# Memory attention: probabilities times values as three f32r products, values split on GpSimd, probabilities on VectorE

## The chip, the core and the metric

The kernel runs on one core of a Trainium2 chip. The metric is the device time of one execution in microseconds (us); a median of several executions is compared. The engines that matter are TensorE (PE in the profile, its weight loads PEld), VectorE (DVE), ScalarE (ACT), GpSimd (POOL) and the queue of SyncE (SPq), which issues the loads of weights. Each runs its own list of instructions in order and waits on semaphores for the others.

## What is computed

Two transformer stacks run one after the other on 256 tokens of width 1024, all in float32. The first has two layers; each is a gated FFN, a mixer with three attention branches whose outputs are gated and merged, and another FFN. The change concerns the memory branch of the mixer: four heads of width 128 attend to 256 memory rows.

```python
def _memory_attention(q, k, v):
    z = jnp.einsum('bhqd,bhkd->bhqk', q, k).astype(jnp.float32) * (q.shape[-1] ** -0.5)
    p = jax.nn.softmax(z, axis=-1)
    return jnp.einsum('bhqk,bhkd->bhqd', p.astype(v.dtype), v)

# in each layer, beside a stick-breaking branch (o_sb) and a forgetting branch (o_fx) of eight heads each
g_sb, g_fx, g_mem = jnp.split(jax.nn.sigmoid(u @ w_gate[l] + b_gate[l]), N_BRANCH, axis=-1)
merged = (g_sb * (_merge_heads(o_sb) @ w_br_sb[l])
          + g_fx * (_merge_heads(o_fx) @ w_br_fox[l])
          + g_mem * (_merge_heads(o_mem) @ w_br_mem[l]))
```

## The kernel before

**Weights.** Every weight matrix streams from memory once, in chunks of up to 128x1024 float32. SyncE loads a chunk into one of four buffers `raw`; ScalarE copies it, rounded to float32r (f32r), into one of six slots `whi` (L578), and VectorE writes the remainder raw - whi into `wlo` (L1103). TensorE then takes three f32r products, high by high, high by low and low by high, in place of one product in full float32. `split_to(c)` marks in ScalarE's and VectorE's lists up to which chunk they have split. A slot is free when TensorE has used its chunk (`w_used`), a raw buffer when VectorE has written wlo.

**The mixer.** For each layer the values V come first, then `NPAIR` = 4 steps, called pairs here (two stick-breaking heads, two forgetting heads and one memory head each), eight in all for two layers. In a pair TensorE does, in this order: feature_chunk(0) and the memory scores (L2040), feature_chunk(1) and (2), the stick-breaking scores, feature_chunk(3), the turned memory probabilities into bank 7 (L1757), gate_chunk(0, 0), the forgetting scores, gate_chunk(0, 1), **probabilities times values** (L2074), gate_chunk(0, 2) and (0, 3), the running sums of the stick-breaking branch (L2086 to L2090), gate_chunk(1, 0) to (1, 3) with the turned forgetting probabilities between, and the outputs of the other two branches. gate_chunk(x, i) writes banks 0 and 1; gate_chunk(1, 0) waits for `gate_done`, that is for VectorE's L1309, which takes the gate of x = 0 out of these banks and adds the bias from `gbias`.

**The places that the change touches.** The memory probabilities are copied out of bank 7 by ScalarE into `mem_pT` (L757), and TensorE multiplies them in full float32 by `vmem`, the values kept in SBUF, for each of the two halves of 128 memory rows (L2074). On VectorE stand around that time `sb_w` (L1356), a weight split, the forgetting scores `fx_s` (L1363), their maxima (L1367), a split, `olo` (L1297), the reciprocal (L1371) of sums that ScalarE's exponentials (L767) yield, the normalisation (L1376), and the gates (L1309). GpSimd masks `sb_sp` (L550), subtracts `sb_lo` (L552) and masks `sb_w` (L554). At the start of a mixer VectorE writes two scaled blocks of ones (L1271, shown as gates) that TensorE turns; GpSimd fills three tiles (L546). SyncE loads a gate bias ahead of each four gate chunks (L469), into three buffers in turn.

The order is that in which each engine's code is written; no scheduler moves it.

Of the kernel before, what the change touches and what calls it, by code (L numbers as in the profile page):

```python
# [7 lines left out]
F32 = mybir.dt.float32  # L8
F32R = mybir.dt.float32r
BF16 = mybir.dt.bfloat16  # L10
ACT = mybir.ActivationFunctionType
ALU = mybir.AluOpType
# [94 lines left out]
def program(nc, A, consts, out):  # L107
    ctx = ExitStack()
    with ctx:
        def sb(name, shape, dt=F32, scope=ctx):  # L110
            return scope.enter_context(nc.sbuf_tensor(name, shape, dt))

        def sem(name):
            return ctx.enter_context(nc.semaphore(name))
# [78 lines left out]
        with ExitStack() as o:  # L193
            ohi, olo = sb("ohi", [P, 3 * NPAIR, TOK], F32R, o), sb("olo", [P, 3 * NPAIR, TOK], F32R, o)
            sb_hi, sb_lo = sb("sb_hi", [P, 2, CAUSAL], F32R, o), sb("sb_lo", [P, 2, CAUSAL], F32R, o)
            exact_r = sb("exact_r", [P, 2 * P], F32R, o)
            with ExitStack() as i:
                sb_e, sb_sp = sb("sb_e", [P, 2, CAUSAL], F32, i), sb("sb_sp", [P, 2, CAUSAL], F32, i)
                sb_w, fx_s = sb("sb_w", [P, 2, CAUSAL], F32, i), sb("fx_s", [P, 2, CAUSAL], F32, i)
                gates = sb("gates", [P, TT, 3 * DM], F32, i)  # L200
                mem_p, mem_pT = sb("mem_p", [P, 512], F32, i), sb("mem_pT", [P, 512], F32, i)
                qs, ks = sb("qs", [P, TOK], F32, i), sb("ks", [P, TOK], F32, i)
                qx = [sb(f"qx{h}", [P, TOK], F32, i) for h in range(2)]
                kx = [sb(f"kx{h}", [P, TOK], F32, i) for h in range(2)]
                crow = sb("crow", [P, TOK], F32, i)
                rstd_bc = sb("rstd_bc", [P, TOK], F32, i)
                V = sb("V", [P, TT, 3 * VB], F32, i)
                gbias = [sb(f"gbias{n}", [P, GB], F32, i) for n in range(3)]
            with ExitStack() as i:
                M = sb("M", [P, TT, DM], F32, i)  # L210
        rb = gates[:, 1, 2 * DM:2 * DM + TT * P].rearrange("p (t n) -> p t n", t=TT)
# [66 lines left out]
        qr0_full, qr_raw, qr_rot, qr_done, qrT_full, qr_ready = (  # L278
            sem(n) for n in ("qr0_full", "qr_raw", "qr_rot", "qr_done", "qrT_full", "qr_ready"))
        group_done = sem("group_done")  # L280
        ls_full, ls_add, ls_max, ls_exp, ls_rec, ls_norm, ls_tp, ls_pt = (
            sem(n) for n in ("ls_full", "ls_add", "ls_max", "ls_exp", "ls_rec", "ls_norm", "ls_tp", "ls_pt"))
        la_full, la_hi, la_lo = sem("la_full"), sem("la_hi"), sem("la_lo")
        y_out, y_stored = sem("y_out"), sem("y_stored")

# [45 lines left out]
        def _(sp):  # L331
# [111 lines left out]
            for l in range(LAYERS):  # L443
                ffn(2 * l, skip=4 if l == 0 else 0)
                if l == 0:
                    for m in range(LAYERS):
                        w = A["w_mem_kv"][m]
                        for n in range(4):
                            load(c_mem + 8 * m + n, cols(w, KT, n * P, P))
                        for j in range(4):  # L450
                            load(c_mem + 8 * m + 4 + j, moving(w, 2 * j, [(MH * P, MH * P)]))
                w = A["w_in"][l]
                v_at = [[(1024, VB)], [(1024 + VB, 512 - VB), (2560, 2 * VB - 512)], [(2560 + 2 * VB - 512, VB)]]
                for i in range(12):
                    load(c_v[l] + i, moving(w, 2 * (i % 4), v_at[i // 4]))
                for h in range(MH):
                    load(c_qm[l] + h, cols(w, KT, 3080 + h * P, P))
                load_gain(3 * l + 1, A["mix_post_g"][l])
                wg = A["w_gate"][l]
                for p in range(NPAIR):  # L460
                    c = c_pair_[l] + 12 * p
                    for n, part_at in enumerate((0, 512, 1536, 2048)):
                        load(c + n, cols(w, KT, part_at + p * P, P))
                    for x in range(2):
                        j = l * 8 + 2 * p + x
                        at = (2 * p + x) * GB
                        if j >= 3:
                            sp.wait_ge(gate_done, 2 * (j - 3) + 2)
                        sp.dma_start(gbias[j % 3][:, :], A["b_gate"][l, at:at + GB].partition_broadcast(P)).then_inc(gb_loaded, 16)  # L469
                        for i in range(4):  # L470
                            load(c + 4 + 4 * x + i, moving(wg, 2 * i, [(at, GB)]))
                wb = [A[n][l] for n in ("w_br_sb", "w_br_fox", "w_br_mem")]
                for i, br in enumerate(BRANCHES):
                    for k in range(4):
                        load(c_br[l] + 4 * i + k, rows_of(wb[br], k))
                for k in range(KT):
                    load(c_wo[l] + k, rows_of(A["w_out"][l], k))
                ffn(2 * l + 1)
# [51 lines left out]
        @block.gpsimd  # L530
        def _(pool):
            diag = lambda t: t[:, :, :].rearrange("p h (a n) -> p h a n", n=P)[:, :, 0:3:2, :]
            mask = before.unsqueeze(1).unsqueeze(1).to_broadcast([P, 2, 2, P])

            def ffn(f):
                for n in range(2, FT):
                    pool.wait_ge(chi_done, wide(f, n) + 1)
                    pool.tensor_tensor(hlo[:, n, :], hid_f[n % 2][:, :], hhi[:, n, :].bitcast(F32), ALU.subtract).then_inc(clo_done, 1)  # L538

            pool.wait_ge(cst_loaded, 32)  # L540
            for l in range(LAYERS):

                ffn(2 * l)
                pool.wait_ge(v_done, 6 * l + 1)
                for n, (tile, value) in enumerate(((qx[0], 1.0), (qx[1], 1.0), (kx[1], 0.0))):
                    pool.memset(tile[:, :], value).then_inc(fx_rows, 1)  # L546
                for p in range(NPAIR):
                    I = l * NPAIR + p
                    pool.wait_ge(sb_dve, I * 2 + 2)
                    pool.tensor_tensor(diag(sb_sp), diag(sb_sp), mask, ALU.mult).then_inc(sb_masked, 1)  # L550
                    pool.wait_ge(sb_high, I + 1)
                    pool.tensor_tensor(sb_lo[:, :, :], sb_sp[:, :, :], sb_hi[:, :, :].bitcast(F32), ALU.subtract).then_inc(sb_split, 1)  # L552
                    pool.wait_ge(sb_exp, I + 1)
                    pool.tensor_tensor(diag(sb_w), diag(sb_w), mask, ALU.mult).then_inc(sb_ready, 1)  # L554
                ffn(2 * l + 1)
            for use in range(2):
                for f in range(FT):
                    pool.wait_ge(chi_done, conv_tile(use, f) + 1)
                    pool.tensor_tensor(hlo[:, f, :], hf[f % 2][:, :], hhi[:, f, :].bitcast(F32), ALU.subtract).then_inc(clo_done, 1)
# [3 lines left out]
        def _(act):  # L563
# [448 lines left out]

            def mla_pT(h):
                act.wait_ge(ls_tp, h + 1)
                act.activation(lpT[h % 4][:, :], bank[4 + h % 2][:, 0:CAUSAL], ACT.Copy).then_inc(ls_pt, 1)

            def mla_high(h):
                act.wait_ge(la_full, h + 1)
# [76 lines left out]
        def _(dve):  # L1095
# [170 lines left out]
            def mixer(l):  # L1266
# [33 lines left out]
                def take_gate(p, x):  # L1300
                    j = l * 8 + 2 * p + x
                    at = (2 * p + x) * GB
                    dve.wait_ge(gb_loaded, 16 * (j + 1))
                    for t in range(TT):
                        if t == 0:
                            dve.wait_ge(gt0_full, j + 1)
                        else:
                            dve.wait_ge(w_used, c_pair_[l] + 12 * p + 8 + 4 * x)
                        dve.scalar_tensor_tensor(gates[:, t, at:at + GB], bank[t][:, 0:GB], stat(b, t, RSTD), gbias[j % 3][:, :],  # L1309
                                                 ALU.mult, ALU.add).then_inc(gate_done, 1)  # L1310

                for p in range(NPAIR):
# [42 lines left out]
                    for h in range(2):  # L1355
                        ins = dve.tensor_tensor(sb_w[:, h, :], bank[2 + h][:, 0:CAUSAL], sb_sp[:, h, :], ALU.subtract)  # L1356
                    ins.then_inc(sb_dve, 1)
                    split_to(c + 3 + SLOTS)

                    dve.wait_ge(fxz_full, I + 1)  # L1360
# [360 lines left out]
        def _(pe):  # L1721
# [223 lines left out]
            def mixer(l):  # L1945
# [66 lines left out]
                for p in range(NPAIR):  # L2012
# [56 lines left out]
                        ins = pe.matmul(bank[4 + h][:, P:CAUSAL], qx[h][r, P:TOK], kx[h][r, 0:TOK], start=True, stop=True)  # L2069
                    ins.then_inc(fxz_full, 1)  # L2070
                    gate_chunk(0, 1)
                    pe.wait_ge(mem_pt, I + 1)
                    for k in range(TT):
                        ins = pe.matmul(bank[6][:, 0:TOK], vmem[l][:, k, p * P:(p + 1) * P], mem_pT[:, k * TOK:(k + 1) * TOK],  # L2074
                                        start=(k == 0), stop=(k == TT - 1))
                    ins.then_inc(o_full[MEM], 1)
                    gate_chunk(0, 2)
                    gate_chunk(0, 3)
# [223 lines left out]
                ins.then_inc(ls_tp, 1)  # L2302

            def mla_values(h):
                pe.wait_ge(ls_pt, h + 1)
                if h >= 2:
                    pe.wait_ge(la_lo, h - 1)
                d = bank[6 + h % 2]
# [116 lines left out]
```

## Time and profile before

| | us |
|---|---|
| median of 3 runs | 1848.41 |
| range of these runs | 1848.38 to 1849.37 |
| the profiled execution | 1848.37 |
| its span, first to last instruction | 1846.6 |

The profile is of one execution. Busy time is the sum over an engine's instructions. A timeline row gives start, duration, engine, line, operation, tiles and count; "x2" joins two instructions that follow each other. In brackets stands how long the engine had been idle and what ended that. TensorE's matmuls overlap, since their durations include the way through the array; what one costs is the step from start to start. A float32 product that isn't f32r shows as two records for one instruction. The granted clock is 1.000 over the whole run, TensorE's level of 2.4 GHz.

### The profile page before, as it was taken

To read this page: it belongs to the slowest core of one execution; us is meant where nothing else is said; L and a number is where in the kernel's file an instruction comes from. 1 tells how busy PE (TensorE), PEld (TensorE's weight loads), DVE (VectorE), ACT (ScalarE), POOL (GpSimd) and SP (SyncE) were. 2 spreads that over 40 slices of the span, in tenths; PEclk is the share of its full clock that TensorE was granted. 3 is DMA by queue.
4 is the path that set the end of the run, shared out by engine and by line. 5 is a ranking of instruction groups with operands and counts; after the bars stand their busy time and mean duration, and the time that the engine had idled before them with its cause. 6 is when DMAs were issued, how large, how long until landed. Compare 5 with 4: busy or idle time off the path is not lost.

```text
span 1846.6 us, 28820 instructions
## 1 busy us (share of the span) xinstructions
PE 1829.8 (99%) x10951; PEld 1633.7 (88%) x10951; DVE 1287.2 (70%) x2040; ACT 1090.1 (59%) x1884; POOL 205.9 (11%) x158
## 2 busy tenths in 40 slices
PE   8999999999999999999999999999999999999998
PEld 7888899998888888888999888888889998889997
DVE  6775747787777567755777778755768765768863
ACT  7665545556666466645555657655557655757653
POOL 0220001110022002200011102210002210001210
PEclk9999999999999999999999999999999999999999
DMA  9765575455576558655654548654747664536753
GB/s 269 208 188 183 168 198 171 140 156 177 171 225 192 189 150 232 186 192 141 191 179 141 188 146 230 190 194 145 220 139 217 190 198 152 176 103 198 204 192 103
DMA packets 435721, 333.94 MB, mean 181 GB/s; under 512 B 25338, under 2 KB 381312, under 8 KB 435584
## 3 DMA queue, kind: packets, MB, share of 16 engines
q1 hardware_dynamic: 435008, 331.57, 59.8%
q8 instruction: 87, 1.43, 0.3%
q10 hardware_dynamic: 576, 0.53, 0.1%
q14 instruction: 50, 0.41, 0.1%
HBM read 330.97 MB, written 1.05 MB: 180 GB/s over the span
## 4 chain that ended last, share of the span: by engine, by line
PE 95%; DVE 2%; ACT 1%; DMA 1%; issue 0%; ACTq 0%; SPq 0%
PE bank L1751 16%; PE bank L1728 14%; PE bank L1730 14%; PE bank L1729 14%; PE bank L1739 7%; PE bank L1741 7%; PE bank L1740 7%; PE bank L1753 7%; PE bank L1757 2%; PE bank L1750 1%; DVE wlo L1103 1%; DVE U L1156 1%; PE bank L2003 0%; PE bank L2069 0%; PE bank L2074 0%
## 5 line engine op out<-in xcount | busy, mean ns | idle before, releaser
L1103 DVE TENSOR_TENSOR wlo<-raw,whi 128x1024 fp32r<-128x1024 f32 (+3 forms) x638 | 761.7, 1201 | 289.6 <-ACT whi L578 280.2
L578 ACT ACTIVATE whi<-raw 128x1024 fp32r<-128x1024 f32 (+3 forms) x638 | 647.0, 1023 | 330.4 <-PE bank L1730 244.8
L1751 PE MATMUL bank<-U,whi 128*128 128x512 f32 x1280 | 438.4, 395 | 0.2 <-DVE wlo L1103 0.2
L1753 PE MATMUL bank<-U,wlo 128*128 128x256 f32 x1120 | 314.6, 281 | 0.0
L1739 PE MATMUL bank<-U,whi 128*128 128x256 f32 x1024 | 289.2, 282 | 0.0
L1741 PE MATMUL bank<-U,wlo 128*128 128x256 f32 x1024 | 286.3, 280 | 0.0
L1740 PE MATMUL bank<-U,whi 128*128 128x256 f32 x1024 | 285.7, 279 | 0.0
L1751 PEld LDWEIGHTS bank<-U,whi 128*128 128x128 f32 x1280 | 229.9, 188 | 42.9 <-DVE wlo L1103 0.7
L1728 PE MATMUL bank<-whi,U 128*128 128x384 f32 (+2 forms) x592 | 219.3, 370 | 2.8 <-DVE U L1156 2.0
L1728 PE MATMUL bank<-whi,hhi 128*128 128x512 f32 x560 | 219.3, 392 | 0.0
L1730 PE MATMUL bank<-wlo,hhi 128*128 128x512 f32 x560 | 218.1, 389 | 0.0
L1729 PE MATMUL bank<-whi,hlo 128*128 128x512 f32 x560 | 217.9, 389 | 0.0
L1753 PEld LDWEIGHTS bank<-U,wlo 128*128 128x128 f32 x1120 | 210.1, 188 | 7.0
L1730 PE MATMUL bank<-wlo,U 128*128 128x384 f32 (+2 forms) x592 | 211.3, 357 | 0.0
L1729 PE MATMUL bank<-whi,U 128*128 128x384 f32 (+2 forms) x592 | 211.2, 357 | 0.0
L1739 PEld LDWEIGHTS bank<-U,whi 128*128 128x128 f32 x1024 | 192.0, 188 | 2.8 <-issue 1.5
L1740 PEld LDWEIGHTS bank<-U,whi 128*128 128x128 f32 x1024 | 192.7, 188 | 0.3
L1741 PEld LDWEIGHTS bank<-U,wlo 128*128 128x128 f32 x1024 | 192.4, 188 | 0.0
L538 POOL TENSOR_TENSOR hlo<-hid_f,hhi 128x256 fp32r<-128x256 f32 x80 | 108.3, 1353 | 598.9 <-ACT hhi L654 598.9
L1730 PEld LDWEIGHTS bank<-wlo,hhi 128*128 128x128 f32 x560 | 105.1, 188 | 22.2
L1729 PEld LDWEIGHTS bank<-whi,hlo 128*128 128x128 f32 x560 | 105.2, 188 | 21.3
L1728 PEld LDWEIGHTS bank<-whi,hhi 128*128 128x128 f32 x560 | 105.1, 188 | 21.0
(307 smaller groups left out, 2365.1 us busy)
## 6 DMA issues: line engine op xcount, KB each, us to landing
raw<-in_ffn_w_up SPq DMA_DIRECT2D x351, 256.0 KB, 3.5
raw<-in_ffn_w_down SPq DMA_DIRECT2D x264, 256.0 KB, 2.9
raw<-in_ffn_w_gate SPq DMA_DIRECT2D x175, 256.0 KB, 3.4
raw<-in_w_gate SPq DMA_DIRECT2D x128, 192.0 KB, 3.0
raw<-in_w_in SPq DMA_DIRECT2D x80, 256.0 KB, 3.5
raw<-in_a_w_in SPq DMA_DIRECT2D x48, 256.0 KB, 3.3
raw<-in_w_mem_kv SPq DMA_DIRECT2D x32, 256.0 KB, 3.3
raw<-in_w_out SPq DMA_DIRECT2D x32, 256.0 KB, 3.0
```

The lines of the kernel that those rows point to most:

```text
L538: pool.tensor_tensor(hlo[:, n, :], hid_f[n % 2][:, :], hhi[:, n, :].bitcast(F32), ALU.subtract).then_inc(clo_done, 1)
L578: act.activation(whi[n % SLOTS][:, 0:w], raw[n % RAW][:, 0:w], ACT.Copy).then_inc(hi_ready, 1)
L1103: dve.tensor_tensor(wlo[n % SLOTS][:, 0:w], raw[n % RAW][:, 0:w], whi[n % SLOTS][:, 0:w].bitcast(F32), ALU.subtract).then_inc(lo_ready, 1)
L1728: pe.matmul(dst, xh, wh, start=start, stop=False)
L1729: pe.matmul(dst, xl, wh, start=False, stop=False)
L1730: return pe.matmul(dst, xh, wl, start=False, stop=stop)
L1739: pe.matmul(dst, wh, xh[:, k, :], start=(k == 0), stop=False, skip_group_check=skip)
L1740: pe.matmul(dst, wh, xl[:, k, :], start=False, stop=False, skip_group_check=skip)
L1741: ins = pe.matmul(dst, wl, xh[:, k, :], start=False, stop=(k == kts - 1), skip_group_check=skip)
L1751: ins = pe.matmul(dst, wh, u2[:, k, :], start=(k == 0), stop=(k == KT - 1))
L1753: pe.matmul(dst[:, 0:TOK], wl, uhi[:, k, :], start=False, stop=False)
L1757: return pe.transpose(dst, src, ident)
```

## The change

The values of a pair are split by GpSimd: `vm_hi` is vmem rounded to f32r, `vm_lo` the remainder. It does that ahead of the pair's first mask, when the previous pair's product has been taken. ScalarE now writes `mem_pT` as f32r, and VectorE writes the remainder of the probabilities, bank 7 - mem_pT, into `mem_pl`, between sb_w and the weight split that follows. TensorE takes three f32r products for each half in place of one float32 product, and waits for both splits. To make room, mem_pl lies where mem_p lies, and there are two gate bias buffers in place of three, so that a bias load waits for the gate two before and not three before. A semaphore is reused for the second stack (mem_pt for ls_pt).

```diff
-                mem_p, mem_pT = sb("mem_p", [P, 512], F32, i), sb("mem_pT", [P, 512], F32, i)
+                with ExitStack() as k:
+                    mem_p = sb("mem_p", [P, 512], F32, k)
+                mem_pl, mem_pT = sb("mem_pl", [P, 512], F32R, i), sb("mem_pT", [P, 512], F32R, i)
...
-                gbias = [sb(f"gbias{n}", [P, GB], F32, i) for n in range(3)]
+                gbias = [sb(f"gbias{n}", [P, GB], F32, i) for n in range(2)]
+                vm_hi, vm_lo = sb("vm_hi", [P, TT, P], F32R, i), sb("vm_lo", [P, TT, P], F32R, i)
...
-                        if j >= 3:
-                            sp.wait_ge(gate_done, 2 * (j - 3) + 2)
-                        sp.dma_start(gbias[j % 3][:, :], A["b_gate"][l, at:at + GB].partition_broadcast(P)).then_inc(gb_loaded, 16)
+                        if j >= 2:
+                            sp.wait_ge(gate_done, 2 * (j - 2) + 2)
+                        sp.dma_start(gbias[j % 2][:, :], A["b_gate"][l, at:at + GB].partition_broadcast(P)).then_inc(gb_loaded, 16)
...
+                    pool.wait_ge(m_taken, 6 * LAYERS)
+                    if I > 0:
+                        pool.wait_ge(o_full[MEM], I)
+                    values = vmem[l][:, :, p * P:(p + 1) * P]
+                    pool.tensor_copy(vm_hi[:, :, :], values).then_inc(vm_split, 1)
+                    pool.wait_ge(vm_split, I * 2 + 1)
+                    pool.tensor_tensor(vm_lo[:, :, :], values, vm_hi[:, :, :].bitcast(F32), ALU.subtract).then_inc(vm_split, 1)
                     pool.wait_ge(sb_dve, I * 2 + 2)
...
                     ins.then_inc(sb_dve, 1)
+                    dve.wait_ge(mem_pt, I * 2 + 1)
+                    dve.tensor_tensor(mem_pl[:, :], bank[7][:, :], mem_pT[:, :].bitcast(F32), ALU.subtract).then_inc(mem_pt, 1)
                     split_to(c + 3 + SLOTS)
...
-                    pe.wait_ge(mem_pt, I + 1)
+                    pe.wait_ge(mem_pt, I * 2 + 2)
+                    pe.wait_ge(vm_split, I * 2 + 2)
                     for k in range(TT):
-                        ins = pe.matmul(bank[6][:, 0:TOK], vmem[l][:, k, p * P:(p + 1) * P], mem_pT[:, k * TOK:(k + 1) * TOK],
-                                        start=(k == 0), stop=(k == TT - 1))
+                        ph, pl = mem_pT[:, k * TOK:(k + 1) * TOK], mem_pl[:, k * TOK:(k + 1) * TOK]
+                        pe.matmul(bank[6][:, 0:TOK], vm_hi[:, k, :], ph, start=(k == 0), stop=False)
+                        pe.matmul(bank[6][:, 0:TOK], vm_hi[:, k, :], pl, start=False, stop=False)
+                        ins = pe.matmul(bank[6][:, 0:TOK], vm_lo[:, k, :], ph, start=False, stop=(k == TT - 1))
                     ins.then_inc(o_full[MEM], 1)
```

On VectorE, in each pair after sb_w. Before:

```order
L1356 TENSOR_TENSOR sb_w<-bank,sb_sp 128x384
L1103 TENSOR_TENSOR wlo<-raw,whi 128x768 [waits hi_ready]
L1363 SCALAR_TENSOR_TENSOR fx_s<-bank,ctok,cst 128x128 [waits fxz_full]
L1363 SCALAR_TENSOR_TENSOR fx_s<-bank,ctok,cst 128x256
L1367 TENSOR_REDUCE fmax<-fx_s 128x2 [waits fx_add]
```

The same place now, where all line numbers are ten or more higher:

```order
L1366 TENSOR_TENSOR sb_w<-bank,sb_sp 128x384
L1369 TENSOR_TENSOR mem_pl<-bank,mem_pT 128x512 [waits mem_pt]
L1113 TENSOR_TENSOR wlo<-raw,whi 128x768 [waits hi_ready]
L1375 SCALAR_TENSOR_TENSOR fx_s<-bank,ctok,cst 128x128 [waits fxz_full]
L1375 SCALAR_TENSOR_TENSOR fx_s<-bank,ctok,cst 128x256
```

One instruction, mem_pl, stands between sb_w and the split; GpSimd's mask waits for sb_w (sb_dve), so it no longer meets the split first.

On TensorE, between gate_chunk(0, 1) and (0, 2). Before:

```order
L1730 MATMUL bank<-wlo,U 128x384
L2074 MATMUL bank<-mem_pT,vmem 128x256 [waits mem_pt]
L2074 MATMUL bank<-mem_pT,vmem 128x256
L1728 MATMUL bank<-whi,U 128x384 [waits lo_ready]
L1729 MATMUL bank<-whi,U 128x384
```

Now:

```order
L1742 MATMUL bank<-wlo,U 128x384
L2088 MATMUL bank<-mem_pT,vm_hi 128x256 [waits vm_split,mem_pt]
L2089 MATMUL bank<-mem_pl,vm_hi 128x256
L2090 MATMUL bank<-mem_pT,vm_lo 128x256
L2088 MATMUL bank<-mem_pT,vm_hi 128x256
L2089 MATMUL bank<-mem_pl,vm_hi 128x256
L2090 MATMUL bank<-mem_pT,vm_lo 128x256
L1740 MATMUL bank<-whi,U 128x384 [waits lo_ready]
```

Two instructions have become six, with one more semaphore to wait for.

On GpSimd, at the start of a mixer. Before:

```order
L546 MEMSET kx 128x256
L550 TENSOR_TENSOR sb_sp<-sb_sp,cst 128x2x2x128 [waits sb_dve]
L552 TENSOR_TENSOR sb_lo<-sb_sp,sb_hi 128x768 [waits sb_high]
L554 TENSOR_TENSOR sb_w<-sb_w,cst 128x2x2x128 [waits sb_exp]
L550 TENSOR_TENSOR sb_sp<-sb_sp,cst 128x2x2x128 [waits sb_dve]
```

Now:

```order
L549 MEMSET kx 128x256
L556 CAST vm_hi<-vmem 128x256 [waits m_taken]
L558 TENSOR_TENSOR vm_lo<-vmem,vm_hi 128x256 [waits vm_split]
L560 TENSOR_TENSOR sb_sp<-sb_sp,cst 128x2x2x128 [waits sb_dve]
L562 TENSOR_TENSOR sb_lo<-sb_sp,sb_hi 128x768 [waits sb_high]
L564 TENSOR_TENSOR sb_w<-sb_w,cst 128x2x2x128 [waits sb_exp]
L556 CAST vm_hi<-vmem 128x256 [waits o_full2,m_taken]
```

The copy and the subtraction stand ahead of each pair's first mask, and so directly behind the previous pair's last one or behind the memsets.

## Rows read from the trace of the kernel before

**Rows 1.** The page's part 1, busy time, share and instructions per engine.

```profile
PE 1829.8 (99%) x10951; PEld 1633.7 (88%) x10951; DVE 1287.2 (70%) x2040; ACT 1090.1 (59%) x1884; POOL 205.9 (11%) x158
```

**Rows 2.** Timeline of TensorE, first pair (start us, duration us, engine, line, operation, tiles).

```profile
301.46 1.02 PE L2074 MATMUL bank<-mem_pT,vmem 128*128 128x256 f32 x4
302.14 0.53 PE L1728 MATMUL bank<-whi,U 128*128 128x384 f32 x1
302.50 0.34 PE L1729 MATMUL bank<-whi,U 128*128 128x384 f32 x1
302.68 0.34 PE L1730 MATMUL bank<-wlo,U 128*128 128x384 f32 x1
```

**Rows 3.** Timeline of TensorE: feature_chunk(2), first and last of 30 matmuls; gate_chunk(1, 0).

```profile
288.25 0.28 PE L1739 MATMUL bank<-U,whi 128*128 128x256 f32 x1
...
291.54 0.28 PE L1741 MATMUL bank<-U,wlo 128*128 128x256 f32 x1
...
307.51 0.35 PE L1728 MATMUL bank<-whi,U 128*128 128x384 f32 x1
```

**Rows 4.** Timeline of VectorE, first pair, from sb_w to the gates of x = 0.

```profile
298.68 1.02 DVE L1356 TENSOR_TENSOR sb_w<-bank,sb_sp 128x384 f32<-128x384 f32 x2
299.61 0.95 DVE L1103 TENSOR_TENSOR wlo<-raw,whi 128x768 fp32r<-128x768 f32 x1
300.48 1.39 DVE L1363 SCALAR_TENSOR_TENSOR fx_s<-bank,ctok,cst 128x128 f32<-128x128 f32 x4
...
302.83 2.48 DVE L1103 TENSOR_TENSOR wlo<-raw,whi 128x768 fp32r<-128x768 f32 x1
...
305.57 0.16 DVE L1371 RECIPROCAL frec<-fsum 128x4 f32<-128x4 f32 x1
...
306.69 1.14 DVE L1309 SCALAR_TENSOR_TENSOR gates<-bank,st,gbias 128x384 f32<-128x384 f32 x2
```

**Rows 5.** Timeline of GpSimd in the same stretch.

```profile
299.78 1.93 POOL L550 TENSOR_TENSOR sb_sp<-sb_sp,cst 128x512 f32<-128x512 f32 x1 [47.60 <-DVE sb_w L1356]
302.66 1.84 POOL L552 TENSOR_TENSOR sb_lo<-sb_sp,sb_hi 128x768 fp32r<-128x768 f32 x1 [0.95 <-ACT sb_hi L761]
```

**Rows 6.** Timeline of ScalarE: first and last row of the four exponentials.

```profile
302.95 0.41 ACT L767 ACTIVATE fx_s<-fx_s,fmax 128x128 f32<-128x128 f32 x1
...
304.63 0.19 ACT L767 ACTIVATION_READ_ACCUMULATOR fx_s<-fx_s,fmax 128x1 f32 x1
```

**Rows 7.** Timeline of VectorE between two stages: 128x512 with a bank as input.

```profile
857.85 0.69 DVE L1128 TENSOR_TENSOR bank<-bank,gpost 128x512 f32<-128x512 f32 x1
```

**Rows 8.** Instructions of L550, L554 and L559: durations in ns, least, median, most.

```profile
L550 POOL TENSOR_TENSOR sb_sp<-sb_sp,cst x8: 1926/1937/1937, 299.8 to 1018.0; 128x512 f32<-128x512 f32 x8
...
L554 POOL TENSOR_TENSOR sb_w<-sb_w,cst x8: 1327/1340/1342, 312.9 to 1031.1; 128x512 f32<-128x512 f32 x8
...
L559 POOL TENSOR_TENSOR hlo<-hf,hhi x44: 737/1276/1480, 1396.3 to 1785.3; 128x256 fp32r<-128x256 f32 x44
```

**Rows 9.** Timeline at the mixer start of layer 1: GpSimd, VectorE, TensorE.

```profile
866.47 0.31 POOL L546 MEMSET kx<- 128x256 f32 x1
...
866.61 1.66 DVE L1103 TENSOR_TENSOR wlo<-raw,whi 128x688 fp32r<-128x688 f32 x2 [2.36 <-ACT whi L578]
868.18 0.48 DVE L1271 TENSOR_SCALAR gates<-cst,st 128x128 f32<-128x128 f32 x2
...
868.72 0.44 PE L1757 MATMUL bank<-cst,gates 128*128 128x128 f32 x2 [0.72 <-DVE gates L1271]
```

**Rows 10.** Timeline of SyncE's queue around two bias loads, and VectorE's second gate.

```profile
309.68 0.50 SPq L469 DMA_DIRECT2D gbias<-in_b_gate  x1
...
316.15 0.43 SPq L469 DMA_DIRECT2D gbias<-in_b_gate  x1
318.23 10.01 SPq L337 DMA_DIRECT2D raw<-in_w_gate  x8
...
316.72 0.62 DVE L1309 SCALAR_TENSOR_TENSOR gates<-bank,st,gbias 128x384 f32<-128x384 f32 x1 [0.36 <-PE bank L1730]
```

More of the change, by code:

```diff
@@ L280, in program @@
         group_done = sem("group_done")
-        ls_full, ls_add, ls_max, ls_exp, ls_rec, ls_norm, ls_tp, ls_pt = (
-            sem(n) for n in ("ls_full", "ls_add", "ls_max", "ls_exp", "ls_rec", "ls_norm", "ls_tp", "ls_pt"))
+        ls_full, ls_add, ls_max, ls_exp, ls_rec, ls_norm, ls_tp, vm_split = (
+            sem(n) for n in ("ls_full", "ls_add", "ls_max", "ls_exp", "ls_rec", "ls_norm", "ls_tp", "vm_split"))
         la_full, la_hi, la_lo = sem("la_full"), sem("la_hi"), sem("la_lo")
@@ L1014, in mla_pT @@
                 act.wait_ge(ls_tp, h + 1)
-                act.activation(lpT[h % 4][:, :], bank[4 + h % 2][:, 0:CAUSAL], ACT.Copy).then_inc(ls_pt, 1)
+                act.activation(lpT[h % 4][:, :], bank[4 + h % 2][:, 0:CAUSAL], ACT.Copy).then_inc(mem_pt, 1)
             def mla_high(h):
@@ L1308, in take_gate @@
                             dve.wait_ge(w_used, c_pair_[l] + 12 * p + 8 + 4 * x)
-                        dve.scalar_tensor_tensor(gates[:, t, at:at + GB], bank[t][:, 0:GB], stat(b, t, RSTD), gbias[j % 3][:, :],
+                        dve.scalar_tensor_tensor(gates[:, t, at:at + GB], bank[t][:, 0:GB], stat(b, t, RSTD), gbias[j % 2][:, :],
                                                  ALU.mult, ALU.add).then_inc(gate_done, 1)
@@ L2304, in mla_values @@
             def mla_values(h):
-                pe.wait_ge(ls_pt, h + 1)
+                pe.wait_ge(mem_pt, 2 * LAYERS * NPAIR + h + 1)
                 if h >= 2:
```

## The prediction

> **What bounds the kernel now.** I read the page's busy times first. The reader is to see one engine that never rests: TensorE is busy 99% of the span, VectorE 70%, ScalarE 59%, GpSimd 11% [rows 1]. So only two things can move the time: what TensorE itself issues, and whether somebody makes it wait. Work added to VectorE or GpSimd is free until it makes one of TensorE's waits end later. For this I then read the timeline of TensorE, VectorE, GpSimd and ScalarE through the first head pair. The other seven pairs repeat it: the mask on GpSimd takes 1926 to 1937 ns in all eight [rows 8].
>
> **Removed and added on TensorE.** Two f32 products per pair appear as four records from 301.46; the next f32r matmul starts at 302.14, but the one after it only at 302.50, where the usual step is 0.18 us (302.50 to 302.68) [rows 2]. So the block costs 302.50 - 301.46 - 0.18 = 0.86 us. In its place stand six f32r matmuls of 256 columns. Thirty of that form stand in one feature chunk, with 29 steps from 288.25 to 291.54, so 0.113 us each [rows 3]; six cost 0.68 us. Saving: 0.18 us a pair, 8 x 0.18 = 1.4 us. The two semaphore waits ahead of them I put at nothing, as mem_pl and vm_hi/vm_lo are ready (next).
>
> **Are the operands ready?** mem_pl reads a bank and one SBUF tile, 128x512; the nearest row is L1128, 128x512 with a bank as input, 0.69 us [rows 7]. It starts where the weight split started, at 299.61, and ends at 300.30, 1.16 us before TensorE asks at 301.46 [rows 2, 4]. The wait for mem_pT in front of it has long ended. vm_hi and vm_lo are made right after the previous pair's last mask on GpSimd, more than ten microseconds before. Cost: nothing.
>
> **What mem_pl pushes back.** Here I expect the loss. Queued behind it on VectorE are a weight split (L1103), the forgetting scores (L1363), their maxima, a second split, the reciprocal and the gates (L1309), and TensorE waits for the first gate before gate_chunk(1, 0), which starts at 307.51 [rows 3]. Before, that gate starts at 306.69 [rows 4] and takes 0.62 us [rows 10], to 307.31: a slack of 0.20 us.
> Step by step, in times of the first pair:
> The first split would start at 299.61 + 0.69 - 0.09 = 300.21 (the next instruction starts 0.09 us ahead of an end: 298.68 + 1.02 against 299.61) [rows 4]. But GpSimd's mask has started at 299.78 [rows 5]. The trace shows what such a pair does: the second split, started at 302.83 while GpSimd subtracts from 302.66 to 304.50, takes 2.48 us in place of 0.95 and ends at 305.31, 0.81 us after GpSimd [rows 4, 5]. And the mask, which now starts 0.17 us behind a split, takes 1.93 us, while one of the same shape on L554 takes 1.34 [rows 5, 8]. So whoever is second stands still. Before, the split was first and GpSimd paid; with mem_pl between, GpSimd is first and VectorE pays. mem_pl itself holds nobody: the scores, also bank plus one SBUF tile, ran from 300.48 beside the mask, which still ended at 301.71.
> The Trainium skill says the same in "SBUF — State Buffer", section "Who interferes with whom": a VectorE instruction with two SBUF inputs and a reading GpSimd instruction exclude each other, and the one that issues first keeps the ports to its end. The trace agrees, with 2.48 us against 0.95.
> So the mask ends at 299.78 + 1.34 = 301.12, the split at 301.93, and the scores start at 301.85 in place of 300.48: 1.37 us late. The four exponentials on ScalarE follow the maxima at once, so they end at 304.63 + 0.19 + 1.37 = 306.19 [rows 6]. The second split is now free: sb_hi and GpSimd's subtraction run 0.59 us earlier and end at 303.91, ahead of the split at 304.20; it ends at 305.15. So the reciprocal waits for the exponentials, not for the split: 306.23 in place of 305.57, 0.66 us late. With it the gate comes at 307.35 and ends at 307.97, TensorE goes on at about 308.01. It arrives at 307.51 - 0.18 = 307.33. Stall: 0.68 us, of which the saving pays 0.18. Net +0.50 us a pair, 8 x 0.50 = +4.0 us.
> Half of the 1.37 us vanishes in slack that is there, since the second split stood still before; that is why the price isn't 1.37.
> What comes later in the pair (sb_w, the second gate, the next pair's first chunk) moves with TensorE's stall and has slack of its own.
>
> **GpSimd's two new instructions.** The subtraction of 128x256 takes 0.74 us at the least (L559's minimum) [rows 8]; the copy lies between the memset of the same size, 0.31 us [rows 9], and that; I take 0.5. In seven of eight pairs they run at the end of the pair before or on an idle engine, where the worst they do is hold a split that lies chunks ahead. At the mixer start of layer 1 it is different: GpSimd's memsets end at 866.78, VectorE runs two splits from 866.61 to 868.27, then the two L1271 that TensorE is already waiting for: it idles 0.72 us up to 868.72 [rows 9]. If the copy slips in between the splits and the subtraction ahead of L1271, these come up to 0.5 + 0.74 = 1.2 us later, all of it TensorE's. Bounds 0 and 1.2 us; I take 1.0, as a waiting GpSimd was served at the end of the split that held it [rows 5]. In layer 0 VectorE is idle at that place.
> On L1271 the rows show no meeting with GpSimd. The Trainium skill, same section, lists tensor_scalar among those that can contend; by it the bound of 1.2 us is reached, without it 0.5.
>
> **The two bias buffers.** SP's load of a bias now waits for the gate two before. For x = 0 that gate ends at about 308.5 with the delay, the load stands at 309.68: no wait. For x = 1 it ends at 316.72 + 0.62 = 317.34, the load stands at 316.15: SP stands 1.2 us, and with 0.43 us of issue is free at 317.77. Queued behind is the next weight load, which starts at 318.23 anyway, as its buffer is not free earlier [rows 10]. Cost: nothing, as long as the cover of 0.46 us holds; both sides move with TensorE's delay.
>
> **Sum.** The profiled execution has a span of 1846.6 us and took 1848.37, the median is 1848.41, so differences carry over. 1848.4 - 1.4 + 5.4 (8 x 0.68) + 1.0 = 1853.4 us.
>
> **Rivals.**
> Absorbed (not slower): the split isn't held by the mask, because VectorE gets the ports although GpSimd began 0.43 us before. Then it runs 300.21 to 301.16, the exponentials end at 305.42, the second split is held until 304.50 as before and ends at 305.31, the reciprocal stays at 305.57, the gate at 307.31 meets TensorE at 307.33. Only the saving is left: 1848.4 - 1.4 + 0 to 1.2, about 1847.6. For it: the slack really is as large as mem_pl's 0.60 us. Against: rows 4 and 5 show the hold in either direction.
> Larger loss: the hold lengthens, because GpSimd also waits for mem_pl and begins only at its end. Then the split ends 0.5 us later still, and since slack is used up all goes to TensorE: +4.0, 1857.4. Against: the scores ran beside the mask.
> The bias load becomes late: SP's wait passes 318.23 and weight loads slip until TensorE sees it. It decides from 0.46 us of further delay; at six or seven places of 0.5 us, 1857. Six weight slots lie between.
> Faster: the three products are worth more than the rows say. The whole block is 8 x 0.86 = 6.9 us, so 3.7 us would need a block of 0.40 us, six matmuls of 0.07. No row has that.
>
> **Chances.** Below 0.2% (3.7 us) a measurement of this kernel can't be told from no change. Main case 0.68, with a range of its own of 1851.2 (stall 0.5, start 0.2) to 1855.4 (stall 0.9, start 1.2); four fifths of it, 0.54, lie above 1852.1. Absorbed 0.22. Larger loss and late bias together 0.08. Faster 0.02. So slower 0.54 + 0.08 = 0.62, same 0.14 + 0.22 = 0.36, faster 0.02. The range takes in the main and the absorbed case, 1847.0 to 1856.0, and leaves out 0.1.
>
> **What would show it.** Right: the split behind mem_pl at about 1.7 us, the mask at 1.34 in place of 1.93, and some 0.7 us of TensorE idle ended by VectorE's gates at each gate_chunk(1, 0); the six matmuls in 0.68 us; TensorE's wait for L1271 in layer 1 near 1.7 us. Wrong: no idle time on TensorE at the gates, or idle time ahead of the six matmuls, or ended by a DMA.

## The result, and the profile after

The changed kernel takes 1854.11 us (median of 9 runs, 1853.61 to 1855.21) against 1848.91 us (9 runs, 1848.38 to 1850.31) of the kernel before on the same chip: ratio 1.0028, 95% interval 1.002 to 1.0036. It is 5.2 us slower; the forecast was 5.0 (1853.4 on a base of 1848.4 us, the median of the first three runs).

The head of the page of the changed kernel, its part 1, and the shares of its chain of work:

```profile
span 1852.4 us, 28891 instructions
```

```profile
PE 1830.7 (99%) x10967; PEld 1634.0 (88%) x10967; DVE 1286.7 (69%) x2048; ACT 1090.4 (59%) x1884; POOL 215.8 (12%) x174
```

```profile
PE 93%; DVE 3%; ACT 2%; issue 1%; DMA 1%; ACTq 0%; SPq 0%
```

Against [rows 1] TensorE is 0.9 us busier and the span 5.8 us longer. So the time isn't in what TensorE does but in what it waits for, and in the chain VectorE and ScalarE have one point more each than before (3% and 2% against 2% and 1%). Where, the table by stage shows. Each row is a stretch in us, its length, and the busy time (and instructions) of PE, PEld, DVE, ACT and POOL; then clock, DMA share and GB/s. Of the kernel before, the four pairs of layer 0, the mixer start of layer 1, and its four pairs:

```profile
285.35:425.67 140.32, 140.32 (x979) 135.38 (x977) 108.74 (x187) 77.40 (x141) 20.50 (x12) 1.00 0.53 160
855.25:896.01 40.76, 39.94 (x287) 39.02 (x286) 28.30 (x54) 27.22 (x53) 0.81 (x3) 1.00 0.79 219
896.01:1036.47 140.46, 140.46 (x979) 135.53 (x977) 108.53 (x187) 77.47 (x141) 20.49 (x12) 1.00 0.52 160
```

The same three stretches of the changed kernel:

```profile
285.44:428.24 142.80, 140.27 (x986) 135.10 (x984) 108.10 (x191) 77.37 (x141) 24.12 (x18) 1.00 0.52 156
857.79:899.24 41.45, 39.96 (x288) 39.05 (x287) 28.58 (x54) 27.03 (x53) 3.00 (x5) 1.00 0.76 208
899.24:1041.82 142.58, 140.08 (x987) 134.88 (x985) 108.38 (x192) 77.25 (x141) 24.12 (x18) 1.00 0.53 160
```

The pairs cost +2.48 and +2.12 us, together 4.60 or 0.58 a pair; the start of layer 1 costs +0.69. In the pairs before, TensorE was busy for the whole of the stretch; now 2.5 us of each are idle. The clock is 1.00 throughout. The remaining 0.5 us of the span lie in stages that the change doesn't touch: 0.09 us ahead of the first pair, and 0.45 us behind the last one (810.58 us to the end of the span in place of 810.13). Both come from one execution of each kernel.

The groups of waits of the changed kernel that matter (what stood and what ended it: us in all, times, the longest of them). Before, no row named the gates of the pairs, and the second one was 0.7 us:

```profile
PE bank L1740 <- DVE gates L1319: 5.0, 8, 0.7
...
PE bank L1769 <- DVE gates L1281: 1.4, 1, 1.4
...
SPq L472 <- DVE gates L1319: 8.0, 6, 1.3
```

Eight waits at gate_chunk(1, 0), one at the mixer start. SyncE's queue now stands 1.3 us at six bias loads (before, 1.3 us at four of them together). No wait of TensorE in the pairs is ended by a DMA; the only one in the run is that for the constants at its start, 2.7 us and 2.8 us before.

Timeline of VectorE in the first pair, from sb_w to the gates, which answers to [rows 4]:

```profile
298.76 1.02 DVE L1366 TENSOR_TENSOR sb_w<-bank,sb_sp 128x384 f32<-128x384 f32 x2
299.70 0.68 DVE L1369 TENSOR_TENSOR mem_pl<-bank,mem_pT 128x512 fp32r<-128x512 f32 x1
300.30 1.67 DVE L1113 TENSOR_TENSOR wlo<-raw,whi 128x768 fp32r<-128x768 f32 x1
301.89 1.38 DVE L1375 SCALAR_TENSOR_TENSOR fx_s<-bank,ctok,cst 128x128 f32<-128x128 f32 x4
...
304.24 0.95 DVE L1113 TENSOR_TENSOR wlo<-raw,whi 128x768 fp32r<-128x768 f32 x1
...
306.25 0.18 DVE L1383 RECIPROCAL frec<-fsum 128x4 f32<-128x4 f32 x1 [0.73 <-ACT fx_s L777]
...
307.39 1.14 DVE L1319 SCALAR_TENSOR_TENSOR gates<-bank,st,gbias 128x384 f32<-128x384 f32 x2
```

And GpSimd's, which answers to [rows 5]:

```profile
299.86 1.29 POOL L560 TENSOR_TENSOR sb_sp<-sb_sp,cst 128x512 f32<-128x512 f32 x1 [46.43 <-DVE sb_w L1366]
302.11 1.86 POOL L562 TENSOR_TENSOR sb_lo<-sb_sp,sb_hi 128x768 fp32r<-128x768 f32 x1 [0.96 <-ACT sb_hi L771]
```

The two have changed places. Before, the split ran first in 0.95 us and the mask took 1.93; now the mask runs first in 1.29 and the split takes 1.67. The scores start at 301.89, 1.41 us later than before (0.09 us of it is the later start of this pair). The second split is free again (0.95, was 2.48), and the reciprocal has waited 0.73 us for ScalarE's exponentials, which before it hadn't. Gate and TensorE follow. TensorE at the product and at gate_chunk(1, 0), with the weight load (PEld) there:

```profile
301.55 0.28 PE L2088 MATMUL bank<-mem_pT,vm_hi 128*128 128x256 f32 x1
...
302.24 0.33 PE L1740 MATMUL bank<-whi,U 128*128 128x384 f32 x1
302.40 0.34 PE L1741 MATMUL bank<-whi,U 128*128 128x384 f32 x1
...
307.22 0.28 PE L2105 MATMUL bank<-sb_lo,exact_r 128*128 128x256 f32 x1
308.15 0.41 PE L1740 MATMUL bank<-whi,U 128*128 128x384 f32 x1 [0.66 <-DVE gates L1319]
308.41 0.34 PE L1741 MATMUL bank<-whi,U 128*128 128x384 f32 x1
```

```profile
308.12 0.19 PEld L1740 LDWEIGHTS bank<-whi,U 128*128 128x128 f32 x1 [0.83 <-issue]
```

The product takes 302.24 - 301.55 = 0.69 us, and the matmul behind it follows after 0.16 instead of the 0.36 of [rows 2]. Then 308.15 - 307.22 = 0.93 us lie between two matmuls where 0.12 is usual. In the other seven pairs it is 0.90 to 0.93.

At the mixer start of layer 1, GpSimd, VectorE and TensorE, answering to [rows 9]:

```profile
869.30 1.01 POOL L556 CAST vm_hi<-vmem 128x256 fp32r<-128x256 f32 x1
870.39 1.23 POOL L558 TENSOR_TENSOR vm_lo<-vmem,vm_hi 128x256 fp32r<-128x256 f32 x1
```

```profile
869.18 1.86 DVE L1113 TENSOR_TENSOR wlo<-raw,whi 128x688 fp32r<-128x688 f32 x2 [2.36 <-ACT whi L588]
870.96 0.94 DVE L1281 TENSOR_SCALAR gates<-cst,st 128x128 f32<-128x128 f32 x2
```

```profile
871.96 0.33 PE L1769 MATMUL bank<-cst,gates 128*128 128x128 f32 x1 [1.40 <-DVE gates L1281]
```

The splits end 0.20 us and L1281 (two instructions) another 0.46 us later than before (0.94 against 0.48): both meet GpSimd's new pair, and TensorE, already waiting, pays all of it.

### The profile page after: what moved, and what is told of

It is laid out like the page before. It is cut to its first block, busy times and chain, and to the rows that moved or that the text cites. A ratio compares the mean times of both kernels' runs of the same rounds, so it can differ in the third digit from the quotient of the medians.

```text
span 1852.4 us, 28891 instructions
## 1 busy us (share of the span) xinstructions
PE 1830.7 (99%) x10967; PEld 1634.0 (88%) x10967; DVE 1286.7 (69%) x2048; ACT 1090.4 (59%) x1884; POOL 215.8 (12%) x174
## 4 chain that ended last, share of the span: by engine, by line
PE 93%; DVE 3%; ACT 2%; issue 1%; DMA 1%; ACTq 0%; SPq 0%
PE bank L1763 16%; PE bank L1740 14%; PE bank L1742 14%; PE bank L1741 14%; PE bank L1751 7%; PE bank L1752 7%; PE bank L1765 7%; PE bank L1753 7%; PE bank L1769 2%; PE bank L1762 1%; DVE wlo L1113 1%; ACT fx_s L777 1%; DVE U L1166 1%; PE bank L2015 0%; PE bank L2081 0%
## 5 line engine op out<-in xcount | busy, mean ns | idle before, releaser
L1740 PEld LDWEIGHTS bank<-whi,U 128*128 128x128 f32 x592 | 111.1, 188 | 19.0 <-issue 7.5
```

The lines of the kernel that those rows point to most:

```text
L1740: pe.matmul(dst, xh, wh, start=start, stop=False)
```

## The experiments

Three questions: is the loss in the pairs GpSimd's being first, or the bias loads or GpSimd's new work; what does the mixer start cost; and is there a version in which the saving remains? The kernel before was timed beside each series. It took 1849.51 us beside the runs with the split first, without mem_pl, with two bias buffers and with the values later, and 1849.01 us beside the other four. Each ratio is to the runs beside it, while the expectations started from 1848.9, 1849.5 or 1854.1.

**Undo the meeting: the split ahead of mem_pl.** Everything else is as in the changed kernel.

```diff
                     ins.then_inc(sb_dve, 1)
+                    split_to(c + 3 + SLOTS)
                     dve.wait_ge(mem_pt, I * 2 + 1)
                     dve.tensor_tensor(mem_pl[:, :], bank[7][:, :], mem_pT[:, :].bitcast(F32), ALU.subtract).then_inc(mem_pt, 1)
-                    split_to(c + 3 + SLOTS)
```

> One line moved: mem_pl stands behind the weight split and no longer ahead of it, so the split starts before GpSimd's mask again. Theory (who starts first keeps the other out): the split takes 0.95 us, the mask 1.93 us, the second split is held as before, the gate ends at its old place, TensorE doesn't wait, and all of the 0.81 us a pair comes back: 1854.1 - 8 x 0.81 = 1847.6 us, below the kernel before. Rival (mem_pl's own 0.60 us on VectorE is what makes the gate late, wherever it stands): 0.60 less the old slack of 0.20 stays, 0.4 us a pair, 1854.1 - 3.2 = 1850.9 us. mem_pl would end 0.3 us before TensorE asks for it; if that isn't enough, idle time shows ahead of the six matmuls.

Measured 1848.94 us, ratio 0.9998 (0.9989 to 1.0007). Its timeline: GpSimd and VectorE, then TensorE's weight load and matmuls at gate_chunk(1, 0).

```profile
299.58 0.95 DVE L1113 TENSOR_TENSOR wlo<-raw,whi 128x768 fp32r<-128x768 f32 x1
...
299.74 1.93 POOL L560 TENSOR_TENSOR sb_sp<-sb_sp,cst 128x512 f32<-128x512 f32 x1 [46.44 <-DVE sb_w L1366]
...
307.40 0.19 PEld L1740 LDWEIGHTS bank<-whi,U 128*128 128x128 f32 x1 [0.23 <-issue]
307.43 0.41 PE L1740 MATMUL bank<-whi,U 128*128 128x384 f32 x1
```

The order of the first meeting is that of before again, and the eight waits are gone from the groups: the place of one VectorE instruction of 0.68 us decides over the loss. A measure for all that follows is how long after the product's first matmul the gate starts: 5.23 us before (306.69 - 301.46), 5.84 in the changed kernel, 5.24 here. The time is that of the kernel before, though, and not 1.3 us below, as I expected (up to 0.6 us of this may be the slower base of the series): TensorE's weight load still stands 0.23 us, and the step to the gate's chunk is 0.30 to 0.34 us in all eight pairs in place of 0.12. The saving of the product brought TensorE to the gate earlier, and the gate wasn't there.

**Leave the mask out.** Order as in the changed kernel, but GpSimd copies one column in place of masking sb_sp.

```diff
-                    pool.tensor_tensor(diag(sb_sp), diag(sb_sp), mask, ALU.mult).then_inc(sb_masked, 1)
+                    pool.tensor_copy(sb_sp[:, 0, 0:1], sb_sp[:, 0, 0:1]).then_inc(sb_masked, 1)
```

> The changed kernel with GpSimd's mask of sb_sp cut down to one column, so that mem_pl stays in its place but nothing of GpSimd is running when the split behind it starts (most of the mask is left out of the computation). Theory (the split is late because GpSimd is first): the split takes 0.95 us in place of 1.67, the exponentials end 0.7 us earlier, the wait at the gates falls from 0.66 us to about 0.05 to 0.2 us, and the time to 1854.1 - 8 x 0.6 = 1849.3 us. Rival (GpSimd has no part in it, mem_pl's own time makes the gate late): no difference, 1854.1.

Measured 1848.11 us, ratio 0.9996 (0.9987 to 1.0005). VectorE and GpSimd:

```profile
300.07 0.68 DVE L1369 TENSOR_TENSOR mem_pl<-bank,mem_pT 128x512 fp32r<-128x512 f32 x1
300.67 0.95 DVE L1113 TENSOR_TENSOR wlo<-raw,whi 128x768 fp32r<-128x768 f32 x1
```

```profile
300.21 0.19 POOL L560 COPY sb_sp<-sb_sp 128x1 f32<-128x1 f32 x1 [46.42 <-DVE sb_w L1366]
```

mem_pl is where it was, and the split behind it takes 0.95 us: without a mask there is nothing to hold it. The gate starts 5.11 us behind the product's first matmul, so mem_pl's own 0.68 us don't make it late. (GpSimd's subtraction is early here too, and has ended before the second split starts, which is then free as well.) The time is 1.2 us less than I expected: the step at the gate is 0.16 to 0.20 us, so 0.7 us a pair come back and not 0.6, and the kernel before ran at 1849.01 in this series. This and the experiment before it show the cause from both sides. It is the order of start that the Trainium skill describes in "SBUF — State Buffer", section "Who interferes with whom"; the four lengths here (0.95 or 1.67 for the split, 1.93 or 1.29 for the mask) agree with it.

**Leave mem_pl and its product out.** VectorE gets back its old list and TensorE has four matmuls in place of six; GpSimd's new work and the two bias buffers stay.

```diff
-                    dve.wait_ge(mem_pt, I * 2 + 1)
-                    dve.tensor_tensor(mem_pl[:, :], bank[7][:, :], mem_pT[:, :].bitcast(F32), ALU.subtract).then_inc(mem_pt, 1)
...
-                        pe.matmul(bank[6][:, 0:TOK], vm_hi[:, k, :], pl, start=False, stop=False)
```

> The changed kernel without mem_pl and without the product that uses it (the low part of the probabilities is left out of the computation); GpSimd's split of the values and the two bias buffers stay. Theory (mem_pl alone makes the gates late): no wait at the gates, four matmuls in place of six save 0.23 us more a pair, the longer wait at the start of layer 1 stays at 1.4 us: 1848.9 - 8 x 0.41 + 0.8 = 1846.4 us. Rival (GpSimd's new instructions or the bias loads cause the waits): the waits of 0.66 us stay, 1854.1 - 8 x 0.23 = 1852.3 us.

Measured 1849.94 us, ratio 1.0004 (0.9995 to 1.0013): a miss, by 3.5 us. The groups of waits still have the gates, at a smaller size:

```profile
PE bank L1738 <- DVE gates L1319: 1.9, 8, 0.3
```

Timeline of VectorE and TensorE there:

```profile
307.09 1.13 DVE L1319 SCALAR_TENSOR_TENSOR gates<-bank,st,gbias 128x384 f32<-128x384 f32 x2
...
307.84 0.41 PE L1738 MATMUL bank<-whi,U 128*128 128x384 f32 x1 [0.28 <-DVE gates L1319]
```

The gate starts 5.25 us behind the product's first matmul, as before, so GpSimd's new work and the bias buffers don't delay it: the wait has another source. The matmul ahead of it starts at 307.28, so the step is 0.56 us, 0.44 above the usual 0.12. From the product's first matmul to the running sums it takes 4.61 us in place of 5.10: TensorE arrives 0.49 us earlier than before, and waits 0.44. In the other pairs both are about 0.39, so that what was saved is given back here. I had counted on 0.20 us of slack that isn't there. In the kernel before, the weight load of gate_chunk(1, 0) was already tied to the gate:

```profile
307.42 0.19 PEld L1728 LDWEIGHTS bank<-whi,U 128*128 128x128 f32 x1
```

The first of the two gate instructions (t = 0) ended at 306.69 + 0.62 = 307.31 [rows 4, 10], and the load began 0.11 us later. It begins 0.11 us later in the changed kernel (308.01, 308.12) and in the one with the split first (307.29, 307.40) as well. In both of these the matmul starts another 0.03 us behind its load (308.15, 307.43). So 0.14 us are needed from the gate's end to the matmul, and of the 0.20 us before, 0.06 were slack. And the first pair, the one that the prediction read, is the exception. In the seven others of the kernel before the matmul starts 0.14 to 0.16 us behind the first gate's end, so there is no slack to speak of, and the step behind that matmul is 0.23 to 0.25 us, where the first pair has 0.19. The second pair, whose gate ended at 342.31 + 0.62 = 342.93:

```profile
343.09 0.40 PE L1728 MATMUL bank<-whi,U 128*128 128x384 f32 x1
343.32 0.34 PE L1729 MATMUL bank<-whi,U 128*128 128x384 f32 x1
```

The gate was just in time in the first pair, and a little late in the others.

**Two bias buffers alone,** in the kernel before.

```diff
-                        if j >= 3:
-                            sp.wait_ge(gate_done, 2 * (j - 3) + 2)
+                        if j >= 2:
+                            sp.wait_ge(gate_done, 2 * (j - 2) + 2)
```

> The kernel before with two gate bias buffers in place of three and nothing else of the change. Theory (the wait on SP ends before the next weight buffer is free): 1848.9, within 0.3 us, though SP waits for the second gate by about 1.2 us in most pairs. Rival (bias loads hold the weights up): TensorE would wait in the pairs, some 0.5 us at up to seven places, 1852.

Measured 1849.4 us, ratio 1.0003 (0.9994 to 1.0012), and no wait of TensorE in the pairs, though SyncE's queue stands at six bias loads here too (7.3 us in all, the longest 1.4). The bias loads cost nothing that shows; the rival falls.

**GpSimd's first pair of instructions later.** It waits until the turned blocks of ones have been taken at the start of each mixer.

```diff
                     pool.wait_ge(m_taken, 6 * LAYERS)
+                    if p == 0:
+                        pool.wait_ge(rb_done, 2 * (3 * l + 2))
```

> The changed kernel, but GpSimd's split of the first pair's values in each layer waits until VectorE has written the two L1281 blocks. Theory (copy and subtraction get between the splits and L1281 in layer 1): TensorE's wait there goes from 1.40 us back to 0.72 and the time falls by 0.7 to 0.9 us, to 1853.3; the waits at the gates stay at 0.66 us each. Rival (the longer wait has another cause, as the mixer start is late anyway): no difference, 1854.1.

Measured 1853.68 us, ratio 1.0023 (1.0013 to 1.0033). The groups of waits:

```profile
PE bank L1742 <- DVE gates L1321: 5.0, 8, 0.7
...
PE bank L1771 <- DVE gates L1283: 0.7, 1, 0.7
```

The wait at the start is back at 0.7 us and the stage at 40.76 us, as before; the pairs keep their waits. The median alone (0.4 us below the changed kernel's) couldn't show 0.7 us; the stage does.

**Take the gate out of the chain.** Gate x = 0 needs only banks 0 and 1, which gate_chunk(0, 3) completes, but it is queued behind the reciprocal, which waits for the exponentials. It is moved ahead of that wait.

```diff
                     head_low(MEM, p)
+                    take_gate(p, 0)
                     dve.wait_ge(fx_exp, I * 4 + 4)
                     dve.reciprocal(frec[:, 0:4], fsum[:, 0:4]).then_inc(fx_rec, 1)
...
                     ins.then_inc(fx_norm, 1)
-                    take_gate(p, 0)
```

> The changed kernel with one step of VectorE moved: in each pair the gates of x = 0 are taken ahead of the reciprocal and the normalisation of the forgetting probabilities, which TensorE needs 3 us later. mem_pl stays ahead of the split and GpSimd's mask stays first. Theory (TensorE waits for the gate alone, and the gate stands only behind the exponentials): the gate ends about 1.7 us earlier, no wait at gate_chunk(1, 0), each set of four pairs takes 140.3 - 4 x 0.18 = 139.6 us or less in place of 142.7, and the time is 1849.5 - 1.4 + 0.7 = 1848.8 us. Rival (VectorE as a whole is late, so that the wait only moves to the turned forgetting probabilities or to the next pair): idle time appears there and the four pairs stay above 141.5 us.

Measured 1847.12 us, ratio 0.9989 (0.9981 to 0.9998). VectorE and TensorE:

```profile
300.59 1.67 DVE L1113 TENSOR_TENSOR wlo<-raw,whi 128x768 fp32r<-128x768 f32 x1
...
305.91 0.62 DVE L1319 SCALAR_TENSOR_TENSOR gates<-bank,st,gbias 128x384 f32<-128x384 f32 x1
```

```profile
307.51 0.28 PE L2105 MATMUL bank<-sb_lo,exact_r 128*128 128x256 f32 x1
307.63 0.33 PE L1740 MATMUL bank<-whi,U 128*128 128x384 f32 x1
```

The split is still held for 1.67 us, and it costs nothing: the first of the two gates ends at 306.53, about 1 us before TensorE asks, and the step is 0.12. The wait hasn't moved elsewhere: TensorE is busy for the whole of both sets of pairs, 139.01 and 138.88 us. The time is 1.7 us below what I expected. The forecast had counted in the whole saving of 0.18 us a pair; 0.5 us of the miss is the faster base of this series, and the rest is that the sets of four pairs are 0.6 and 0.7 us shorter than the 139.6 expected. What that consists of is taken up further down.

**Both of these.**

> The same with GpSimd's split of each layer's first values held until the two L1281 blocks are written. Theory: both losses are gone and the saving of 0.18 us a pair is whole; 1849.5 - 1.4 = 1848.1 us, four pairs in 139.6 us, layer 1's start in 13.47 us. Rival: the two losses aren't independent and the sum isn't reached.

Measured 1846.34 us, ratio 0.9984 (0.9976 to 0.9993): the best of all, 2.7 us below the kernel before (1849.01 beside it) and 7.8 below the changed one, which was timed in another series. It is 1.8 us below what I expected, for the same reasons as the run before. Its stages:

```profile
285.90:424.92 139.02, 139.02 (x987) 134.56 (x985) 108.22 (x191) 77.16 (x141) 24.12 (x18) 1.00 0.53 160
854.47:895.24 40.77, 39.95 (x288) 39.02 (x287) 27.82 (x54) 27.03 (x53) 3.26 (x5) 1.00 0.78 213
895.24:1034.10 138.86, 138.86 (x986) 134.41 (x984) 108.20 (x192) 77.40 (x141) 24.00 (x18) 1.00 0.53 162
```

TensorE has no idle time in the pairs, and they are 1.30 and 1.60 us shorter than before.

**The same move in the kernel before,** to see whether it is a gain of its own.

> The kernel before with only that step of VectorE moved. In the kernel before TensorE's weight load for gate_chunk(1, 0) starts 0.11 us after the gate's end, as it does in the kernels where it waits. Theory (the slack was about zero there, not 0.20 us, but not below): no difference to the kernel before, 1849.5, four pairs within 0.3 us of 140.3. Rival (the gate held TensorE up already): four pairs fall by some tenths of a us each, 1848.5.

Measured 1848.61 us, ratio 0.9998 (0.9989 to 1.0007): no difference that a median can show, and the sets of pairs, 140.26 and 140.21 us, lie within the 0.3 us. The trace does show one, at the second pair's gate_chunk(1, 0):

```profile
343.80 0.34 PE L1728 MATMUL bank<-whi,U 128*128 128x384 f32 x1
343.97 0.34 PE L1729 MATMUL bank<-whi,U 128*128 128x384 f32 x1
```

The step behind the gate's first matmul is 0.17 us where it was 0.23, and 0.17 or 0.18 in all eight pairs. So the rival was right in kind: the gate did hold TensorE up, by about 0.07 us in seven pairs, some 0.5 us together. That is too small for the medians, which differ by 0.4. The move gains more than this only with the change.

## Why the prediction came true, and where it was off

- **The saving on TensorE: right.** The product takes 0.69 us (0.68 to 0.71 in all pairs), the forecast was 0.68, and the slow second step behind it is gone. With the two gate chunks that follow, the stretch from the product's first matmul to the running sums takes 4.84 to 4.87 us in the eight pairs, where it took 5.05 to 5.10: 0.2 us saved.
- **mem_pl in time, values in time: right.** No idle time ahead of the six matmuls; mem_pl ended at 300.38, 1.2 us before TensorE asked.
- **Who is first: right, and shown** by the two experiments on it. The forecast had the mask at 1.34 us (measured 1.29), the split's end at 301.93 (301.97), the reciprocal at 306.23 (306.25) and the gate at 307.35 (307.39); this pair starts 0.09 us later than before, so in its own time all of it came some 0.05 us earlier than forecast.
- **The slack: mis-sized.** "a slack of 0.20 us" was reckoned from the gate's end to the matmul's start, and TensorE was to go on 0.04 us behind the delayed gate. It takes 0.14, as the weight load comes first: the row to read was the load's, not the matmul's. And the 0.20 us, read in the first pair, don't stand for the other seven, where it is 0.14 to 0.16 us, all of it needed. The stall is 0.93 - 0.12 = 0.81 us in the first pair, not 0.68: 0.10 from this, 0.08 because the steps behind the product are shorter too and TensorE is there sooner, less the 0.05 by which the gate is early. In the other pairs it is 0.78 to 0.81. Less some 0.2 saved, a pair loses 0.6; measured 0.58, forecast 0.50, so 4.6 us in place of 4.0. The same term, the other way round, made me expect times 1.3 and 3.5 us too low for the kernels with the split first and without mem_pl; up to 0.6 us of each may be the base, which was 1849.51 and not 1848.9.
- **The mixer start: right in kind, too large.** +0.69 us in the place of 1.0. The copy did slip in at the splits, but held them by 0.20 us only, and the subtraction held L1281 by 0.46. That L1281, a tensor_scalar, can be held was the part that no row before showed: 0.94 us against 0.48. The rule of the Trainium skill, same page and section as above, that tensor_scalar is among what can contend, agrees with it.
- **The bias buffers: right.** They cost nothing, alone and in the changed kernel, though SyncE's queue stands 1.3 us at six loads.
- **The sum.** 4.6 + 0.7 = 5.3 us against 5.2 measured; the forecast's 4.0 + 1.0. The two errors, 0.6 us up and 0.3 us down, have opposite signs, so the sum fits better than its terms do; that part is luck.

Open: the pairs of the best version are 0.33 (layer 0) and 0.40 us (layer 1) shorter than those of before, and the product with the chunks behind it explains 0.2. The freed step at the gate is another 0.06 to 0.08 in seven pairs. Most of the rest are chunks whose steps are all slightly longer, without a wait: 48 matmuls of two feature chunks take 5.93 us in the third pair of both layers before, and 5.72 or 5.73 in the best version, and some chunks of 24 take 4.42 in place of 4.34, or 2.93 in place of 2.83. Neither the stall nor the product decides over these: in the changed kernel and in the one before with the gate moved the 5.93 is there, in the one with the split first it is in no pair, and with two bias buffers alone in one layer only. No run here tells what does.

## What to carry to other kernels

An instruction on an engine with time to spare can cost more than it takes, or nothing: it decides who starts first where two engines meet, and so whose instruction stands still. Slack is measured at the waiting engine's first instruction behind the wait (here the weight load, not the matmul); where that starts right behind the event, there is next to none, and every saving ahead of it is given back there. Then look at what stands between the event and its inputs: an instruction that is ready but queued behind another's wait can be moved ahead of it, and here this alone turned a change of +5.2 us into one of -1.9, each against the kernel before in its own series.

## What the runs showed of the hardware that was not expected

- From the end of VectorE's gate to TensorE's weight load 0.10 to 0.12 us pass, in every pair of this case in which the load waits for the gate. With the stall gone TensorE isn't at its pace at once: 308.15 to 308.41 is 0.26 us, where 0.17 is usual. A gate that is only just too late, as in seven pairs of the kernel before, shows in no row of waits, but in this one step of 0.23 to 0.25 us.
- GpSimd's copy of 128x256 to f32r takes 0.40 us undisturbed and up to 1.41 when it meets VectorE (1.70 with the values later, where it starts 0.2 us behind the first of two splits in a row); a subtraction of the same size takes 0.74 and up to 1.23. Of the changed kernel, all eight of each (ns; least, median, most):

```profile
L556 POOL CAST vm_hi<-vmem x8: 396/1392/1407, 252.2 to 1001.4; 128x256 fp32r<-128x256 f32 x8
...
L558 POOL TENSOR_TENSOR vm_lo<-vmem,vm_hi x8: 736/740/1233, 252.7 to 1002.9; 128x256 fp32r<-128x256 f32 x8
```

- A float32 product between f32r ones costs TensorE something after its end too: the 24 matmuls behind it take 4.37 to 4.42 us, and 4.15 to 4.16 behind the six f32r ones. The late second step of [rows 2] is 0.18 of it; the others are spread.
